# A reordered tail of the second gated attention in a one-core hybrid block kernel

## The reference

```python
xw, xa, xg = ...                                   # low-rank inputs of decay, a and gate
decay = exp(-exp(-softplus(-(w0 + tanh(xw) @ w2)) - 0.5))
a     = sigmoid(a0 + xa @ a2)
g_r   = sigmoid(xg) @ g2
kk    = rk * k_k;  kk = kk / max(norm of kk over each head, 1e-12)
rk    = rk * (1 + (a - 1) * k_a)
o_r   = rwkv7_scan(rr, decay, rk, rv, kk, a)       # S = S*decay - (S kk)(kk a)^T + v k^T; o = S r
o_g   = chunked_gated_linear_attention(gq, gk, gv, log_a)   # "gla"; "hgrn" has the same form
y_gla = rms(o_g) * silu(gg)
```

## Time and profile before

| | us |
|---|---|
| median of 3 runs (lowest to highest) | 1684.16 (1682.77 to 1685.19) |
| the profiled execution's own time | 1687.16 |
| its span | 1685.2 |
| PE busy | 1650.3 (98%) |
| DVE busy | 861.3 (51%) |
| ACT busy | 669.0 (40%) |
| POOL busy | 124.7 (7%) |
| mean granted PE clock | 0.987 of full |
| the stretch of the change | about 1144 to 1238 of the span |

### The profile page before, as it was taken

One profiled execution on the slowest core, in us unless ns is written; L12 is line 12 of the kernel. 1 busy time (PEld: TensorE's weight loads), 2 busy tenths in 40 slices (PEclk: granted clock), 3 DMA queues, 4 the chain that ended last, 5 costly groups with the idle time before them and its releaser, 6 DMA issues.

```text
span 1685.2 us, 23809 instructions
## 1 busy us (share of the span) xinstructions
PE 1650.3 (98%) x9540; PEld 1338.2 (79%) x9540; DVE 861.3 (51%) x1170; ACT 669.0 (40%) x1017; POOL 124.7 (7%) x126
## 2 busy tenths in 40 slices
PE   9999999999999999999999999998999999999997
PEld 6877778877777888888888878887877888888886
DVE  6733445542444565444433478577556554444333
ACT  6145565314656433233222355346333433333221
POOL 0001001000100110000000310000410200000000
PEclk9999999999999999999999999997899999999999
DMA  5412212331221223332233422220002232232331
GB/s 180 154 63 76 88 51 88 113 125 63 75 77 53 98 85 103 100 101 90 88 103 94 141 76 63 63 66 18 3 23 86 88 101 92 96 97 85 103 98 56
DMA packets 40750, 144.14 MB, mean 86 GB/s; under 512 B 4816, under 2 KB 4832, under 8 KB 40256
## 3 DMA queue, kind: packets, MB, share of 16 engines
q1 hardware_dynamic: 37296, 131.61, 24.7%
q0 software_dynamic: 2192, 8.87, 1.6%
q10 hardware_dynamic: 1152, 2.14, 0.4%
HBM read 140.50 MB, written 2.10 MB: 85 GB/s over the span
## 4 chain that ended last, share of the span: by engine, by line
PE 85%; DVE 8%; ACT 5%; issue 1%; POOL 0%; DMA 0%; DVEq 0%; ACTq 0%; SPq 0%; POOLq 0%
PE bank L497 25%; PE bank L499 24%; PE bank L498 24%; PE bank L479 3%; PE bank L1017 2%; PE bank L485 1%; DVE sb_w_low L1230 1%; PE bank L664 1%; PE bank L728 1%; PE bank L707 1%; ACT sb_w_high L1999 1%; DVE sb_E L1230 1%; PE bank L862 1%; DVE sb_near L1644 1%; DMA sb_x<-xT 0%
## 5 line engine op out<-in xcount | busy, mean ns | idle before, releaser
L1230 DVE TENSOR_TENSOR sb_w_low<-sb_raw,sb_w_high 128x1024 fp32r<-128x1024 f32 (+1 forms) x253 | 310.9, 1229 | 368.0 <-ACT sb_w_high L1999 361.5
L497 PE MATMUL bank<-sb_xg_high,sb_w_high 128*128 128x512 f32 x1176 | 465.6, 396 | 2.0 <-DVE sb_w_low L1230 1.4
L499 PE MATMUL bank<-sb_xg_high,sb_w_low 128*128 128x512 f32 x1176 | 459.0, 390 | 0.0
L498 PE MATMUL bank<-sb_xg_low,sb_w_high 128*128 128x512 f32 x1176 | 458.5, 390 | 0.0
L1999 ACT ACTIVATE sb_w_high<-sb_raw 128x1024 fp32r<-128x1024 f32 (+1 forms) x253 | 263.3, 1041 | 349.1 <-PE bank L499 325.1
L497 PEld LDWEIGHTS bank<-sb_xg_high,sb_w_high 128*128 128x128 f32 x1176 | 221.1, 188 | 65.3 <-issue 15.8
L499 PEld LDWEIGHTS bank<-sb_xg_high,sb_w_low 128*128 128x128 f32 x1176 | 221.0, 188 | 47.1
L498 PEld LDWEIGHTS bank<-sb_xg_low,sb_w_high 128*128 128x128 f32 x1176 | 221.3, 188 | 44.3 <-issue 0.2
L499 PE MATMUL bank<-sb_h_high,sb_w_low 128*128 128x512 f32 x352 | 136.9, 389 | 0.0
L497 PE MATMUL bank<-sb_h_high,sb_w_high 128*128 128x512 f32 x352 | 136.9, 389 | 0.0
L498 PE MATMUL bank<-sb_h_low,sb_w_high 128*128 128x512 f32 x352 | 136.9, 389 | 0.0
(11 more groups left out here) (343 smaller groups left out, 1995.4 us busy)
## 6 DMA issues: line engine op xcount, KB each, us to landing
sb_raw<-w_ffn_in SPq DMA_DIRECT2D x88, 512.0 KB, 3.5
sb_raw<-w_ffn_out SPq DMA_DIRECT2D x32, 512.0 KB, 3.5
sb_raw<-w_tok SPq DMA_DIRECT2D x24, 512.0 KB, 3.5
sb_raw<-w_mix_f SPq DMA_DIRECT2D x18, 512.0 KB, 3.5
sb_raw<-w_rot SPq DMA_DIRECT2D x16, 512.0 KB, 3.6
sb_raw<-w_qk SPq DMA_DIRECT2D x16, 512.0 KB, 3.4
sb_raw<-w_out SPq DMA_DIRECT2D x16, 512.0 KB, 3.5
sb_raw<-w_ffn_out SPq DMA_DIRECT2D x16, 384.0 KB, 3.1
```

The costliest lines, as they stand in the source:

```text
L497: e.matmul(out, w[0], v[0], start=first, stop=False)
L498: e.matmul(out, w[0], v[1], start=False, stop=False)
L499: return e.matmul(out, w[1], v[0], start=False, stop=last)
L1230: e.tensor_tensor(out, a, b, op).then_inc(*v.up(*signal))
```

## The change

What moves, engine by engine:

- **Keys' norms.** The squares of the keys are taken by ACT after the fifth rwkv tile, into the room of `y_rwkv`, not in step 6 into kI; PE sums them in step 6, DVE floors them in step 6, ACT spreads them in step 7 ahead of the sigmoids, PE turns them in step 8.
- **Tanh** of the low-rank levels goes after the seventh rwkv tile instead of after the eighth; the products that read it move ahead of the scores of level 1.
- **Gate.** ACT's silu for gla goes from call 4 to call 2.
- **Decays moved by a token.** kkE was keys times exp(-(sum - sigma)), with its own subtraction and exponential. Now each chunk's first key is copied and the others are multiplied by the decay of the token before: the subtraction and one exponential go, a small copy comes.
- **Gram products** wait for kkE (and with it bI) alone, later ones for kI and rE; rE is made after the masks of the inverse.
- **Presets.** X is laid down before the second half of `mixed` is awaited, XT right behind it, and the landing of that half after them; DVE waits head by head.
- **End of gla.** ACT's root and DVE's last three operations go behind the first level of the inverse; "near done" is marked at level 64.
- **PE's filler** `keep_busy` goes from 3 + 1 products to 2, and the gate's low-rank products go behind the scores of level 128.

Cut to its core:

```diff
@@ tensor_engine
-                    keep_busy(3)
+                    fill(len(ORDER))
+                    keep_busy(2)
                 scores(n)
-            if name == "gla":
-                keep_busy(1)
-            fill(len(ORDER))
+            if name == "hgrn":
+                fill(len(ORDER))
...
         def operand_steps():
-            yield
...
-                    group(banks[i][:, at:at + 2], [(m.kI[:, f, blk(t)], ...)], "key norm")
+                    group(banks[i][:, at:at + 2], [(m.key_sq[:, f, blk(t)], ...)], "key norm")
+            yield
+            yield
+            (key turned, from m.key_sq)
             yield
             (gate out)
...
-        before_products = ("rE",)
+        operand_of = {"AT": "kkE", "X": "kkE", "A_ak": "kI", "M_rk": "rE", "M_rb": "rE"}
-            p.wait_ge(*of(*before_products))
+            p.wait_ge(*of(operand_of[what]))
@@ vector_engine
+                    if ORDER[n - 1] == 64:
+                        v.mark("near done", name)
...
                 reduce(ms, split(squares), "mean square", name)
+                yield
                 v.wait_ge(*of("root", name))
...
-            tt(m.tmp, m.cum, m.sigma, ALU.subtract, "sigma before")
...
-            tt(m.kkE, kk, m.tmp, ALU.mult, *STEP)
...
+            ts(out[:, :, 0:1], keys[:, :, 0:1], 1.0, None, ALU.mult, ALU.bypass, *STEP)
+            tt(out[:, :, 1:], keys[:, :, 1:], fades[:, :, 0:CHUNK - 1], ALU.mult, "kkE")
+            tt(m.kI, rk, eI, ALU.mult, "kI")
...
-        v.wait_ge(*of("X preset"))
-        v.wait_ge(*of("XT preset"))
         for h in HEADS:
             masked("AT", m.AT[:, h, :], h, mem.table("before"))
+            v.wait_ge(*of("XT preset", h))
...
-        finish_gla()
+        tt(m.rE, m.mixed[:, 0:2, :], m.eB, ALU.mult, "rE")
+        finishing = finish_gla()
+        next(finishing)
...
+            if size == 2:
+                next(finishing)
@@ scalar_engine
+                if name == "gla" and half:
+                    preset("XT", m.XT)
                 act(m.y_tok[name][:, 2 * half:2 * half + 2, :], ..., "mixed landed", name, half)
+                if name == "gla" and not half:
+                    a.wait_ge(*of("factors read", "gla", len(ORDER) - 1))
+                    preset("X", m.X)
...
         def operand_steps():
+            yield
+            a.wait_ge(*of("key inverse"))
+            act(heads(flat(m.key_sq)), ..., "key spread")
             a.wait_ge(*of("rwkv mixed", 7))
-            act(m.mixed[0:64, 6, :], m.mixed[0:64, 6, :], "rwkv tanh", func=ACT.Tanh)
...
-            act(m.tmp, m.tmp, *STEP, func=ACT.Exp, scale=-HALF_E)
             act(m.rE, m.cum, "rwkv exps", func=ACT.Exp, scale=HALF_E)
...
-        finish_gla()
...
+                    if size == 2 and h == 2:
+                        finish_gla()
```

More of the change, by code:

```diff
@@ L80 @@
                                "rwkv own,X preset,XT preset"),
-        ("rwkv operands by V", "key floored,key scaled,sigma summed,sigma before,rE,rwkv landed,rwkv mixed"),
+        ("rwkv operands by V", "key floored,key scaled,sigma summed,bonus products,kkE,kI,rE,rwkv landed,rwkv mixed"),
         ("inverse by T", "AT product,X product,A_ak product,Gv product,M_rk product,M_rb product,W1 product,"
@@ L1656, in linear_attention @@
                     fill(n + 1)
-            v.mark("near done", name)
             fill(len(ORDER))
```

81 lines of the change are left out of this document (43 added, 38 removed).

## The result

| | before | changed |
|---|---|---|
| median, us | 1684.16 (1682.77 to 1686.86, 5 runs) | 1695.47 (1692.26 to 1700.15, 5 runs) |
| profiled execution; its span | 1687.16; 1685.2 | 1698.57; 1696.8 |
| PE busy, mean granted clock | 1650.3, 0.987 | 1653.2, 0.983 |

The medians lie 11.3 us apart (0.7%), where +2.5 was forecast in a range that ended at +6.8. The page's two rows for PE say where to look: one slice (1145 to 1188 us) fell from 8 to 7 tenths busy and from 7 to 6 tenths of clock.

A forecast was written before the change was run, and what follows sets the result against it. PE, busy 98% of the span, was taken as the bound, with changes only between 1138 and 1222 us. +1.6 − 1.4 − 2.7 + 4.5 = +2.0, with +0.5 +2.5: 1684.16 to 1686.7 us; 8-in-10 range 1680.0 to 1691.0.

The forecast's parts named there:

- The tanh wait and what takes its place: Ahead of level 64: PE's 3.03 us tanh wait goes, a sigmoid wait of some 7.4 us comes, level 64 at 1158.9.
- From there to the first Gram product: Level 64 to the first Gram product: far ends near 1178.4, then 6.2 us of `mixed`; +1.6 us, bounds 0 and +4.7.
- the sentence on the filler: Ahead of `mixed`: 2 filler products instead of 4 cost nothing, since PE waits there for ACT.
- the rivals: Alternatives for the whole: slower 1689.4 (0.33), faster 1680.2 (0.16), bank wait not as it looks 1681.6 (0.12).
- The half clock over level 64: Level 64 behind the new wait: half clock expected, 3.68 us; at full clock 2.00 us, giving the term's bound 0.
- Presets and Gram products: First Gram product to first Pm product: earlier presets gain 0, as PE is busy there; bounds −0.4 and +0.4 us.
- Pm and level 2: In level 2: Pm no longer behind ACT's root, −1.4 us; full clock in level 2, −2.7 us.
- The second new wait: In level 4: waiting for y made delays the first step 3.2 us, head 2's product more; +4.5 us in all.
- rival (a): Slower: PE's clock falls in level 4, costing 3.2 us; +5.2 in all, 1689.4, or 1691.0; chance 0.33.
- the sum's +0.5: In level 4: allowance of +0.5 us for a possible clock fall after the second wait, which could cost up to 3.2.

The follow-up runs named there:

- e14: The changed kernel with PE's low-rank products and key norms behind the scores of level 1 again, as before; median 1693.51 us.
- e13: The changed kernel with the filler ahead of `mixed` as before, three and one products in place of two; median 1689.55 us.
- e5: The changed kernel with one unread 128x512 product on PE between the halves of `mixed`; median 1690.73 us.
- e10: The changed kernel with unread products ahead of the key norms, at level 64 and in `mixed`, later readers of y, tanh in ACT's idle time; median 1685.73 us.
- e9: The changed kernel with POOL's gate steps one level later and ACT's first two Gv behind level 4's first two Pm; median 1687.83 us.
- e6: The changed kernel with unread products at three places: one ahead of the key norms, six at level 64, one in `mixed`; median 1690.08 us.
- e1: The changed kernel with ACT's spread of the keys' norms behind the sigmoids again; median 1696.24 us.
- e2: The changed kernel with the end of gla where it was, ahead of level 2; median 1697.46 us.
- e4: The changed kernel with seven unread 128x512 products on PE in the wait at level 64; median 1693.47 us.
- e3: The changed kernel with the spread of the norms behind the sigmoids and the end of gla where it was; median 1690.43 us.
- e11: The changed kernel with unread products (four at level 64), later readers of y, tanh in ACT's idle time, key spread behind the sigmoids; profiled 1686.36, others 1691.45 to 1694.99 us.
- e15: The changed kernel with PE order undone, later readers of y, tanh in ACT's idle time, unread products at level 64 and in `mixed`; median 1682.72 us.
- e17: The changed kernel with PE order and filler as before, later readers of y, tanh in ACT's idle time, no added unread products; median 1683.27 us.
- e7: The kernel before with only the tanh sooner, after the seventh projection tile; median 1690.07 us against 1686.69 beside it.

## Why the prediction was wrong

**The tanh wait and what takes its place: right.** 6.7 us for 7.4, level 64 at 1158.77 for 1158.9. That the wait is the bank of "sigma in" is shown by e14, where it goes with the order. One small step was missed: the scores of level 1 do not follow in one run but wait 1.20 for DVE's copies, and the clock fell there, at 1150.0, ahead of the long wait.

**From there to the first Gram product: wrong, and here the forecast failed.** Two steps failed. One is the sentence on the filler, which priced it at nothing: "2 products instead of 4 in the idle time ahead of `mixed`; nothing, since PE waits there for ACT." Restored alone (e13) they are worth 5.9 us between the medians. They hid no dependency; they took up the idle for far. Without them an idle of 1.23 there was followed by 17 us at half clock, in which most of `mixed`, the Gram products and the turned operands all are (e5 and e13 show it from two sides). The other is the term itself: +1.6, with the second half of `mixed` at full clock. It took 10.2 (1178.63 to 1188.83) and not 6.2, and the first Gram product came 6.9 later than before by the table (5.8 in the times of the span). Of these, 3.4 are far and 3.5 the clock in `mixed`. A fall inside `mixed` was not among the rivals, though the profile before had one right behind it, among the bonus sums, at 1186.

Far itself landed where the forecast had it, at 1178.49 for 1178.4, and that is in part luck. This execution stood 1.1 sooner at the common event, and 0.75 of that was lost again on the way: ACT's exponentials of level 64 start 43.7 after the event, before 43.0. The delay begins at the third rwkv tile (9.8 for 8.1), behind the gate's silu, which the change put ahead of that tile's weights and the forecast left out. It is the same in e10, so it is not the tanh's place; it was not undone alone. The half clock over level 64 the forecast had right, with 0 as the bound without it: e10, at full clock there, has the first Gram product at 78.8, 0.8 later than before.

**Presets and Gram products: 0, right as far as seen.** DVE's first mask began 2.6 after the first Gram product, not 4.4, and nothing followed: from Gram to the first Pm product it is 12.6 us, at half clock for 8.7, against 10.1, and 10.1 again in e5 (81.0 to 91.1), where that half clock is 3 us. This part of the change was not undone alone.

**Pm and level 2: right in kind.** Level 2 took 8.66 (1201.38 to 1210.04), against 12.63: −4.0 for −1.4 − 2.7 = −4.1. The idle for Pm is 0.62 for 2.62.

**The second new wait: right, but its rival (a) came and not the sum's +0.5.** From product to step it is 4.54 (4.3 predicted), to the product of head 2 6.76 (6.6). The clock fell, as rival (a) says: 7.4 us more than before from level 4's first product to the turned y, for +4.5 + 0.5 in the sum and 4.5 + 3.2 = 7.7 in the rival. e9 gives 4.2 of it back.

**The sum of the parts as they came:** +6.9, −1.5 and +7.4 make +12.7, where the text had +1.6, −4.1 and +5.0. The middle would be −4.0 but for half clock from the Gram products on. The two medians lie 11.3 apart. Without the half clock in `mixed` (e5, e6, e13) the changed kernel is at 1689.6 to 1690.7, inside the range that was given.

**What stays open.** Among the profiled executions the changed kernel, e1, e2, e4, e9 and e14 had the long half clock in `mixed`, and their lists of waits have 0.9 to 2.8 us for sb_far at the products of `mixed`; e3 (0.48), e5, e6, e10, e11, e13 and e15 to e17 had neither. What decides between two executions of one kernel, as in e1, e9, e14 and e15, no run shows. Nor do traces show that the other long executions have their half clock in `mixed`. Their mean granted clock does show that they have more of it: in e1, e9, e14 and e17 it is 0.983 to 0.985 for the long ones and 0.987 to 0.993 for the short ones, in e15 0.988 for 0.990 to 0.993. Some 17 us more at half clock are 0.005 of an execution's mean, and the distance of the groups, 8 to 10 us, fits as well.

## What to carry to other kernels

Before a filler product is priced at nothing, look at the stretch behind it: narrow products that follow an idle microsecond may run their whole length at half clock, and the wait itself is the small part of the bill (here 1.2 us of idle, and 4.7 to 5.9 us back once it was filled). A filler takes time at whatever clock it gets, and can outlast the wait that it fills: seven products took 8.79 us in a hole of 6.7. A wait of the busiest engine is worth its length only if nothing further on waits for the same chain of other engines; taking away PE's longest wait alone made the kernel before slower (e7), as waits of 2.89 and 2.43 us came at other places. When a result is moved later, move its readers too, since an engine that waits in order holds up all that is queued behind the wait.

## What was not expected of the hardware

- In the changed kernel the half clock came at 1150.0, ahead of the wait of 6.7: 0.9 us after an idle of 1.20 that stands behind the key norms of two columns each (16 records, 1.95 us). In the kernel before it fell at 1186.0 behind bonus sums of two columns, with PE busy throughout.
- It then stayed for 20 us, while PE was busy for 12.17 of them, and in `mixed` for 16.5 us with PE busy for all of them. In e4, with wide unread products in the hole, it was over after 7 us.
- Executions of one kernel on one chip fall in two groups 8 to 10 us apart (e1, e9, e14, e15), the long ones at a mean granted clock lower by 0.004 to 0.005. An edit that moves the median by 6 us may only have moved executions from one group to the other. With only five executions of the changed kernel this could not be seen; with eight to twelve of the others it could.
